# Head of a two-block fp32 kernel: input also loaded transposed, first norm applied behind the products, weight stream begun with a gate block

## The chip, the cores and the metric

The kernel runs on one core of one Trainium2 chip. The metric is the device time of one execution in microseconds (us). TensorE (PE) multiplies, ScalarE (ACT) and VectorE (DVE) work on vectors, GpSimd (POOL) does small work and issues some transfers, and SyncE (SP) issues the stream of weights.

## The reference

Two transformer blocks over 256 tokens of width 2048, all in float32. What matters here is the head of the first:

```
h   = rms_norm(x, g_mix_pre)          # x * rsqrt(mean(x*x) + eps) * g
z   = h @ w_in                        # columns: fox q,k,v,f | hgrn q,f,i,g
y1  = forgetting_attention(q, k, v, f + b)        # 8 heads
o   = hgrn2_recurrence(q_b, (1-lb)*sigmoid(-f_b), i_b, log_f)   # lb is 0 for a depth of 1
y2  = rms_norm(o, g_o) * silu(g_b)
h   = x + rms_norm(concat(y1, y2) @ w_out, g_mix_post)
```

Then come a gated feed-forward layer with a short convolution, a gated embedding, neighbourhood attention and a squared-ReLU layer. The root of a token is one number for a row of `x`, so it may be applied to the product's row (or column, where the product stands transposed) in place of the input's.

## The kernel before

All weights (some 430 MB) are read once, in 832 **slots** of at most 512 KB, fetched by SP in a fixed order into a ring of four buffers `RAW`. For exact enough products each fp32 value is split in two: ACT copies `RAW` to `HI` in the reduced format, DVE subtracts to get `LO`; PE then does three products (hi by hi, lo by hi, hi by lo). `HI` and `LO` are rings of five. ACT and DVE split slot j + 4 (`LEAD`) when they come to slot j, and ACT waits until PE is done with slot j - 1 for it. The input of a product is held transposed and in two parts too (`XT[:, k, 0]` and `XT[:, k, 1]`, k the 128-row chunk of the width).

A **block** is a set of slots that sum into one of two PSUM tensors `main0` and `main1`, in turn: `w` blocks (256 columns, 4 slots; the weights stand as the left operand) and `x` blocks (512 or 344 columns, 8 slots). `layout` lists them: hgrn f, q (`hf`, `hq`), v (`vh`), gate (`gh`), fox v (`vf`, three blocks of 344 columns, slots 32 to 55, called narrow below), then the second half of hgrn, fox q and k (`qf`, `kf`), and so on. After its last slot a block is evacuated by ACT and DVE (`evacuate`); a `w` block by `w_half` (ACT) and `w_sum` (DVE).

Work beside the stream is written out by hand in `stages`: `put(mid, j, ...)` makes every engine do a step after slot j. The recurrence of each half of the heads is done in this way: `h_abs`, `h_log`, `h_key`, `h_scan`, then eight levels of `h_decay` (DVE and POOL, then an exponential on ACT), `h_weigh` (DVE and POOL) and `h_score` (PE, and a masked copy on DVE), three slots a level, then `h_far`, `h_out`, `h_rms`, `h_gated`, `h_turn`. The score of level L reads what `h_weigh` of level L - 1 wrote. The first half starts at slot 16, the second at slot 72; the attention steps `f_score` and others go from slot 88 on.

The start is serial: x (2 MB) is loaded in four parts, ACT squares all of it, DVE and ACT make the root, both scale 512 columns each (`norm`), PE transposes them (`turn`), ACT and DVE write the two parts of `XT`, and then the first product can begin.

Of the kernel before, what the change touches and what calls it, by code (L numbers as in the profile page):

```python
# [71 lines left out]
def layout(a):  # L72
# [57 lines left out]
def stages():  # L130
# [7 lines left out]
    put(mid, 0, "norm", 0, 3)  # L138
    for kp, j in ((4, 0), (5, 0), (6, 1), (7, 1)):
        put(mid, j, "turn", 0, kp)  # L140

    for hf, j0 in enumerate((16, 72)):
# [5 lines left out]
        for lvl in range(1, 9):  # L148
            at = j0 + 7 + 3 * (lvl - 1)
# [6 lines left out]
        put(mid, j0 + 32, "h_out", hf)  # L156
        put(mid, j0 + 34, "h_rms", hf)
        put(mid, (j0 + 34, 120)[hf], "h_gated", hf)
        put(mid, (j0 + 37, 122)[hf], "h_turn", hf)
# [25 lines left out]
    put(mid, 156, "spread")  # L185
    put(mid, 155, "rb")
# [46 lines left out]
def small_banks(blocks, mid, end, early):  # L233
# [11 lines left out]
    def stage(what):  # L245
# [36 lines left out]
        elif name == "spread":  # L282
            take(("spread",), ("a_rb", 1))
# [6 lines left out]
    for kp in range(4):  # L290
        stage(("turn", 0, kp))
# [13 lines left out]
def program(nc, a):  # L305
    ctx = ExitStack()
    with ctx:
# [53 lines left out]
        XIN, NA0 = ar(12800, 2, D), ar(0, 2, D)  # L361
# [16 lines left out]
        MSKF = ar(8192, 8, 128)  # L378
        hss, hl, hr = small(32, 8), small(160, 8), small(168, 8)
# [52 lines left out]
        def freed(k):  # L432

            if k[0] in ("hf", "hq", "qf", "kf", "gate", "up", "m1"):
                return "v_wy", wth[k] + 1
            if k[0] in ("vh", "gh", "e"):
# [17 lines left out]
        wants = {k: freed(paired[i - 2]) for i, k in enumerate(paired) if i > 1}  # L454

# [32 lines left out]
        def sync_engine(eng):  # L488
# [3 lines left out]
            for t in range(2):  # L492
                for c in range(2):
                    cs = slice(c * 1024, c * 1024 + 1024)
                    L.e.dma_start(XIN[:, t, cs], xv[:, t, cs]).then_inc(S(f"d_x{t}{c}"), 16)

            def fetch(j):
# [3 lines left out]
                if j >= NRAW:  # L501
                    L.wait_ge(S("v_lo"), j - NRAW + 1)
                L.e.dma_start(dst, ap).then_inc(S(f"d_raw{i}"), 16)
# [9 lines left out]
            for j in range(len(slot)):  # L513
                fetch(j)
                if j == 140:
# [17 lines left out]
        def tensor_engine(eng):  # L533
# [10 lines left out]
            def turn(ph, kp):  # L544
                X = (NA0, H, H, H, H)[ph]
                out = take("turn", ph, kp)
                if kp == 0 and ph == 0:
                    L.wait_ge(S("d_id"), 16)
                if ph == 0:
                    L.wait_ge(S("v_n"), kp // 2 + 1)  # L550
                    L.wait_ge(S("a_n"), kp // 2 + 1)
                else:
                    L.wait_ge(S("v_h"), stream(ph - 1, kp // 2, 1))
                for q in range(2):
                    for t in range(2):
                        k = 2 * kp + q
                        x = L.e.transpose(out[:, (2 * q + t) * 128:(2 * q + t) * 128 + 128], X[:, t, k * 128:k * 128 + 128], ident)  # L557
# [12 lines left out]
            def h_score(hf, lvl):  # L570
                A, B = (Kh, Qh) if lvl == 0 else (wbuf[(lvl - 1) % 2],) * 2
                for t in range(2):
                    out = take("h_score", hf, lvl, t)
                    if lvl == 0:
                        L.wait_ge(S("a_hk"), hf + 1)
                        L.wait_ge(S("v_wy"), wth["hq", hf, 1] + 1)
# [40 lines left out]
            def f_score(h):  # L617
# [3 lines left out]
                L.wait_ge(S("v_wy"), wth["kf", hp] + 1)  # L621
# [58 lines left out]
            def spread():  # L680

                out = take("spread")
                L.wait_ge(S("v_dg"), 2)
                for t in range(2):
                    x = mm(out[:, t * 128:t * 128 + 128], ones[:, 0:128], DG[:, t, :], True, True)
# [24 lines left out]
            def x_slot(b, j, cs, out, first, last):  # L710
                hi, lo = parts(HI, j, b.n), parts(LO, j, b.n)
                A = XT if b.src == "x" else YT
                for q, c in enumerate(cs):
                    L.wait_ge(S(inputs(b, c)[0]), inputs(b, c)[1])
                    if q == 0:
# [40 lines left out]
            for kp in range(4):  # L756
                turn(0, kp)
# [20 lines left out]
        def scalar_engine(eng):  # L778
# [5 lines left out]
            def warm():  # L784
                L.wait_ge(S("v_eps"), 1)
                act(small(31, 1), epsc, ACT.Sqrt)

            def split(j):
                i, m = j % NRAW, len(slot[j][2]) * width[j]
                L.wait_ge(S(f"d_raw{i}"), 16 * (j // NRAW + 1))  # L790
                if j >= NHI:
                    L.wait_ge(S("p_use"), j - NHI + 1)
                act(HI[:, j % NHI, 0:m], RAW[:, i, 0:m], ACT.Copy).then_inc(S("a_hi"), 1)
# [5 lines left out]
            def norm(ph, c):  # L799
                cs = slice(c * 512, c * 512 + 512)  # L800
                L.wait_ge(S("v_rs"), 1)
                act(NA0[:, 1, cs], XIN[:, 1, cs], ACT.Copy, scale=rs[:, 1:2]).then_inc(S("a_n"), 1)

            def turn(ph, kp):
                out = banks[bank["turn", ph, kp]]
                L.wait_ge(S("p_xp"), turned(ph, kp))
                if ph == 0 and kp == 0:
# [17 lines left out]
            def h_abs(hf):  # L825
                L.wait_ge(S("v_wy"), wth["hf", hf, 1] + 1)
# [60 lines left out]
            def sq(inst, c):  # L887

                cs = slice(c * 512, c * 512 + 512)
                for t in range(2):  # L890
                    L.wait_ge(S("v_h"), stream(inst, c, t))
                    if c:
                        L.wait_ge(S("a_sq"), 8 + 8 * inst + 2 * c + t - 1)
# [4 lines left out]
            def root2(inst):  # L898
                root(2 + 2 * inst)

            def rb():
                L.wait_ge(S("p_rb"), 1)
                act(RB, banks[bank["spread",]][:, 0:256], ACT.Copy).then_inc(S("a_rb"), 1)

            def gate(t):
# [5 lines left out]
                L.wait_ge(S("v_rs"), 5)  # L911
# [829 lines left out]
```

## Time and profile before

| what | value |
|---|---|
| median of 3 runs | 2440.12 us (2440.0 to 2440.66) |
| the profiled execution, its own time | 2439.97 us |
| its span, first to last instruction | 2438.2 us |
| PE busy in the span | 2414.8 us, 99% |
| DVE busy, ACT busy | 1522.6 us (62%), 1221.8 us (50%) |
| transfers | 449.19 MB, mean 184 GB/s |

The time outside the span is 1.77 us. The profile's clock column (PEclk) reads full speed throughout.

### The profile page before, as it was taken

Reading aid. Unit: us, or ns where it says so; the run is one execution under the profiler, and the core shown is the slowest. Engines: PE = TensorE matmul, PEld = TensorE weight load, DVE = VectorE, ACT = ScalarE, POOL = GpSimd, SP = SyncE. Lnnn points to the kernel's source line nnn. Section 1 sums busy time; section 2 is a strip of 40 time slices with the busy share of each in tenths; the row PEclk is TensorE's granted clock in tenths of the full one; section 3 lists DMA queues with packets and bytes.
Section 4 is the critical chain, followed back from the end, with each engine's and each line's share of the span. In section 5 each row is a group of like instructions: output and inputs, shape, how many; then the busy total and the mean of one; then the engine's idle time right before and its main releaser. Section 6 shows DMA issues by size and latency. Waiting matters only on the chain.

```text
span 2438.2 us, 30545 instructions
## 1 busy us (share of the span) xinstructions
PE 2414.8 (99%) x12380; PEld 2054.9 (84%) x12380; DVE 1522.6 (62%) x1777; ACT 1221.8 (50%) x1603; POOL 111.5 (5%) x121
## 2 busy tenths in 40 slices
PE   7999999999999999999999999999999999999999
PEld 6898888788888888888877888888888888888887
DVE  5675765577657657767666666665665565554554
ACT  5554454465545545545565655554543443443442
POOL 0210410000000000000000211000000000000000
PEclk9999999999999999999999999999999999999999
DMA  8456565656655655555655655555566656566664
GB/s 245 136 163 181 147 201 168 205 160 203 199 181 177 205 180 192 196 180 183 216 191 164 190 175 174 164 164 182 180 199 191 190 187 193 183 194 193 189 196 151
DMA packets 325821, 449.19 MB, mean 184 GB/s; under 512 B 14240, under 2 KB 209056, under 8 KB 325040
## 3 DMA queue, kind: packets, MB, share of 16 engines
q1 hardware_dynamic: 323424, 438.42, 57.2%
q0 software_dynamic: 2256, 8.81, 1.2%
q8 instruction: 98, 1.61, 0.3%
q14 instruction: 43, 0.35, 0.0%
HBM read 445.08 MB, written 2.10 MB: 183 GB/s over the span
## 4 chain that ended last, share of the span: by engine, by line
PE 94%; DVE 4%; ACT 1%; issue 1%; DMA 0%; POOL 0%; SPq 0%; ACTq 0%; DVEq 0%
PE main L537 90%; PE aux L537 3%; DVE LO L1107 2%; DVE AR L1107 1%; ACT HI L782 1%; PE aux L557 1%; DVE AR L1257 0%; DMA AR<-in_x 0%; ACT AR L782 0%; PE aux L651 0%; PE aux L669 0%; DVE XT L1110 0%; POOL AR L1561 0%; DVE AR L1226 0%; DVE AR L1227 0%
## 5 line engine op out<-in xcount | busy, mean ns | idle before, releaser
L1107 DVE TENSOR_TENSOR LO<-RAW,HI 128x1024 fp32r<-128x1024 f32 (+1 forms) x832 | 1005.9, 1229 | 631.2 <-ACT HI L782 630.3
L782 ACT ACTIVATE HI<-RAW 128x1024 fp32r<-128x1024 f32 (+1 forms) x832 | 849.5, 1046 | 623.5 <-PE main L537 587.8
L537 PE MATMUL main<-XT,HI 128*128 128x512 f32 x2944 | 1037.1, 397 | 0.7 <-DVE LO L1107 0.7
L537 PE MATMUL main<-XT,LO 128*128 128x256 f32 x2944 | 825.6, 280 | 0.0
L537 PE MATMUL main<-HI,YT 128*128 128x512 f32 x2240 | 693.4, 389 | 0.0
L537 PEld LDWEIGHTS main<-XT,HI 128*128 128x128 f32 x2944 | 552.4, 188 | 132.3 <-issue 0.9
L537 PEld LDWEIGHTS main<-XT,LO 128*128 128x128 f32 x2944 | 556.2, 189 | 0.3
L537 PEld LDWEIGHTS main<-HI,YT 128*128 128x128 f32 x2240 | 420.5, 188 | 87.5
L537 PE MATMUL main<-HI,XT 128*128 128x512 f32 (+1 forms) x1472 | 456.5, 385 | 1.7 <-DVE LO L1107 1.6
L537 PE MATMUL main<-LO,YT 128*128 128x512 f32 x1120 | 435.8, 389 | 0.0
L537 PEld LDWEIGHTS main<-HI,XT 128*128 128x128 f32 x1472 | 273.8, 188 | 52.9 <-issue 1.5
L537 PE MATMUL main<-LO,XT 128*128 128x512 f32 (+1 forms) x736 | 279.9, 380 | 0.0
L537 PEld LDWEIGHTS main<-LO,YT 128*128 128x128 f32 x1120 | 210.3, 188 | 43.1
L782 ACT ACTIVATE AR<-AR 128x512 f32<-128x512 f32 (+7 forms) x187 | 108.6, 583 | 169.3 <-DVE AR L1107 84.5
L537 PEld LDWEIGHTS main<-LO,XT 128*128 128x128 f32 x736 | 138.5, 188 | 23.7
L782 ACT ACTIVATE AR<-main 128x512 f32<-128x512 f32 (+3 forms) x113 | 72.0, 638 | 150.7 <-PE main L537 150.4
L1110 DVE SCALAR_TENSOR_TENSOR AR<-main,AR 128x512 f32<-128x512 f32 (+1 forms) x125 | 86.3, 701 | 94.4 <-ACT AR L782 78.8
L1107 DVE TENSOR_TENSOR AR<-AR 128x512 f32<-128x512 f32 (+2 forms) x151 | 106.8, 714 | 25.5 <-ACT AR L782 22.4
L1110 DVE SCALAR_TENSOR_TENSOR AR<-AR,COL 128x256 f32<-128x256 f32 x176 | 74.8, 481 | 32.9 <-ACT AR L782 32.9
L537 PE MATMUL aux<-AR 128*128 128x128 f32 (+2 forms) x528 | 89.7, 316 | 4.0 <-DVE AR L1107 2.8
L537 PEld LDWEIGHTS aux<-AR 128*128 128x128 f32 x528 | 75.3, 191 | 13.4 <-issue 6.6
L782 ACT ACTIVATE AR<-AR,COL 128x256 f32<-128x256 f32 x88 | 48.2, 595 | 68.7 <-DVE AR L1107 68.7
(82 smaller groups left out, 685.6 us busy)
## 6 DMA issues: line engine op xcount, KB each, us to landing
RAW<-in_mlp_w SPq DMA_DIRECT2D x256, 512.0 KB, 4.1
RAW<-in_w_up SPq DMA_DIRECT2D x176, 512.0 KB, 4.8
RAW<-in_w_in SPq DMA_DIRECT2D x96, 512.0 KB, 3.7
RAW<-in_na_w_qkv SPq DMA_DIRECT2D x96, 512.0 KB, 4.2
RAW<-in_w_down SPq DMA_DIRECT2D x88, 512.0 KB, 4.7
RAW<-in_w_out SPq DMA_DIRECT2D x32, 512.0 KB, 4.3
RAW<-in_w_ple_gate SPq DMA_DIRECT2D x32, 512.0 KB, 4.5
RAW<-in_na_w_o SPq DMA_DIRECT2D x32, 512.0 KB, 4.2
```

The costliest lines, as they stand in the source:

```text
L537: return L.e.matmul(out, l, r, start=start, stop=stop, skip_group_check=True)
L557: x = L.e.transpose(out[:, (2 * q + t) * 128:(2 * q + t) * 128 + 128], X[:, t, k * 128:k * 128 + 128], ident)
L782: return L.e.activation(out, x, f, **kw)
L1107: return L.e.tensor_tensor(out, x, y, op)
L1110: return L.e.scalar_tensor_tensor(out, x, s, y, op0, op1, **kw)
```

## The change

The host also passes `xT`, x transposed and laid out so that a partition's row of two chunks is 2 KB. SP loads it in eight parts of 256 KB, each ahead of the weights of a slot; the first slot's weights come in two halves. ACT and DVE make `XT` straight from it with the gains alone; there are no transposes and no norm ahead of the products. The gain columns come by a small transfer that ACT itself issues.

x itself is loaded behind slots 8 to 11; ACT squares it at slots 10 and 11 (`sq0`), POOL makes the root by a power (`root0`), and PE spreads it over the partitions at slot 15 (`spread`, 0), for which ACT copies the result to `RB0`. Row-wise products (`vh`, `gh`, `vf`) get the root as ACT's scale, in two operations where there was one; transposed ones (`hf`, `hq`, `qf`, `kf`) by one more DVE product (`rooted`). The stream begins with block `gh` 0, which is kept as it is until the root is there (`gate0`). The first half's recurrence moves from slot 16 to 24, its levels and those of the second half one slot later after the first, and `f_score` to `f_out` one slot later. POOL's small loads move from the start behind slots 0, 3 and 16.

```diff
@@ layout
     w_in = a["w_in"]
+    add("x", w_in, OG, 512, allk, "x", "gh", 0)
     for hf in range(2):
...
         if hf == 0:
-            add("x", w_in, OG, 512, allk, "x", "gh", 0)
             for b in range(3):
@@ stages
-    put(mid, 0, "norm", 0, 3)
-    for kp, j in ((4, 0), (5, 0), (6, 1), (7, 1)):
-        put(mid, j, "turn", 0, kp)
+    put(mid, 0, "first_loads")
+    put(mid, 3, "more_loads")
+    put(mid, 10, "sq0", 0)
+    put(mid, 11, "sq0", 1)
+    put(mid, 11, "root0")
+    put(mid, 15, "spread", 0)
+    put(mid, 15, "rb", 0)
+    put(mid, 16, "gate0")
+    put(mid, 16, "last_loads")
-    for hf, j0 in enumerate((16, 72)):
+    for hf, j0 in enumerate((24, 72)):
...
-            at = j0 + 7 + 3 * (lvl - 1)
+            at = j0 + 8 + 3 * (lvl - 1)
...
-        for what, j in (("f_decay", j0 - 6), ("f_score", j0 + 1), ("f_norm", j0 + 2), ("f_turn", j0 + 4), ("f_out", j0 + 6)):
+        for what, j in (("f_decay", j0 - 6), ("f_score", j0 + 2), ("f_norm", j0 + 3), ("f_turn", j0 + 5), ("f_out", j0 + 7)):
@@ sync_engine
             for j in range(len(slot)):
+                if j < 4:
+                    turned_input(j)
                 fetch(j)
+                if j in (3, 4):
+                    turned_input(2 * j - 2)
+                    turned_input(2 * j - 1)
+                if 8 <= j < 12:
+                    input_rows((j - 8) // 2, j % 2)
@@ tensor_engine
+                    if j == 0 and q == 0:
+                        L.wait_ge(S("v_x0"), 1)
+                        L.wait_ge(S("v_l0"), 1)
@@ scalar_engine
+            def turned_input(kp, q):
+                k = 2 * kp + q
+                L.wait_ge(S("d_g0"), 16)
+                L.wait_ge(S(f"d_t{kp}"), 16)
+                act(XT[:, k, 0, :], XTR[:, k, :], ACT.Copy, scale=COL[:, P_MIX + k:P_MIX + k + 1]).then_inc(S("a_x0"), 1)
...
+            def sq0(t):
+                for c in range(2):
+                    L.wait_ge(S(f"d_x{t}{c}"), 16)
+                    xs = XIN[:, t, c * 1024:c * 1024 + 1024]
+                    act(xs, xs, ACT.Square, scale=MEAN, accum_out=ss2[:, t, 2 + c:3 + c]).then_inc(S("a_s0"), 1)
@@ vector_engine
+            def rooted(b, dst, n):
+                L.wait_ge(S("a_rb"), 1)
+                L.wait_ge(S("v_wy"), wth[b.what] + 1)
+                tt(dst, dst, bc(RB0, 1, n), ALU.mult).then_inc(S("v_ws"), 1)
```

How the engines' orders change is shown at three places. First ACT, from its first instruction; `d_x`, `d_raw`, `d_t`, `d_g0` and `d_w0` are transfers' semaphores (x, a slot, a part of xT, the gains, the first half slot). Before:

```order
L782 ACTIVATE AR<-AR 128x512 [waits d_x00]
L782 ACTIVATE AR<-AR 128x512
L782 ACTIVATE AR<-AR 128x512 [waits d_x01]
...
L782 ACTIVATE AR<-AR 128x2 [waits v_ms]
L782 ACTIVATE AR<-AR 128x512 [waits v_rs]
L782 ACTIVATE AR<-AR 128x512
L782 ACTIVATE HI<-RAW 128x1024 [waits d_raw0]
L782 ACTIVATE XT<-aux,COL 128x256 [waits d_col,p_xp]
```

The same place after:

```order
L1125 DMA COL<-in_cols 128x16
L802 ACT_TABLE_LOAD
L802 ACTIVATE AR<-AR 128x1 [waits v_eps]
L802 ACTIVATE XT<-AR,COL 128x256 [waits d_t0,d_g0]
L802 ACTIVATE HI<-RAW 128x512 [waits d_w0]
L802 ACTIVATE XT<-AR,COL 128x256
L802 ACTIVATE HI<-RAW 128x512 [waits d_raw0]
L802 ACTIVATE XT<-AR,COL 128x256 [waits d_t1]
L802 ACTIVATE XT<-AR,COL 128x256
L802 ACTIVATE HI<-RAW 128x1024 [waits d_raw1]
```

Eleven instructions ahead of the first split (eight squares, the root and two scalings) are gone, and the split of slot 0 stands in two halves. Second PE, from its first instruction; before:

```order
L557 MATMUL aux<-CST,AR 128x128 [waits a_n,v_n,d_id]
L557 MATMUL aux<-CST,AR 128x128 x7
L557 MATMUL aux<-CST,AR 128x128 [waits a_n,v_n]
L557 MATMUL aux<-CST,AR 128x128 x7
L537 MATMUL main<-XT,HI 128x512 [waits v_lo,v_xl]
```

and after:

```order
L562 MATMUL main<-HI,XT 128x512 [waits v_l0,v_x0]
L562 MATMUL main<-LO,XT 128x512
L562 MATMUL main<-HI,XT 128x512 x2
L562 MATMUL main<-LO,XT 128x512
L562 MATMUL main<-HI,XT 128x512
L562 MATMUL main<-HI,XT 128x512 [waits v_lo,v_xl]
```

The 32 transposes (16 here, 8 behind each of slots 0 and 1) are gone. Third DVE in the second half's recurrence, from the first level's decay to the fox block `qf` 0 (`128x256x2` is level 1, `128x128x4` level 2). Before:

```order
L1107 TENSOR_TENSOR AR<-AR 128x512 [waits v_wy,a_hx]
L1107 TENSOR_TENSOR LO<-RAW,HI 128x1024 [waits a_hi]
L1107 TENSOR_TENSOR AR<-AR 128x256x2
...
L1107 TENSOR_TENSOR AR<-AR 128x128x4
L1107 TENSOR_TENSOR LO<-RAW,HI 128x1024 [waits a_hi]
L1107 TENSOR_TENSOR AR<-AR 128x128x4 [waits a_hx]
L1110 SCALAR_TENSOR_TENSOR AR<-main,AR 128x512 [waits a_wt,a_n,v_n]
L1107 TENSOR_TENSOR LO<-RAW,HI 128x1024 [waits a_hi]
```

and after:

```order
L1144 TENSOR_TENSOR AR<-AR 128x512 [waits v_ws,a_hx]
L1144 TENSOR_TENSOR LO<-RAW,HI 128x1024 [waits a_hi] x2
L1144 TENSOR_TENSOR AR<-AR 128x256x2
...
L1144 TENSOR_TENSOR AR<-AR 128x128x4
L1147 SCALAR_TENSOR_TENSOR AR<-main,AR 128x512 [waits a_wt]
L1144 TENSOR_TENSOR AR<-AR 128x512 [waits v_wy]
L1144 TENSOR_TENSOR LO<-RAW,HI 128x1024 [waits a_hi]
L1144 TENSOR_TENSOR AR<-AR 128x128x4 [waits a_hx]
```

One more split stands ahead of level 1, and the evacuation of `qf` 0 is followed by the product with the root and stands ahead of the wait for the exponential.

## Rows read from the trace of the kernel before

**Rows 1.** Waits of PE, all of the span: us in total, times, longest.
```profile
PE aux L557 <- ACT AR L782: 12.5, 1, 12.5
```
**Rows 2.** Timeline of the start: start us, us, instruction [idle before, releaser].
```profile
0.73 1.81 SPq L495 DMA_DIRECT2D AR<-in_x  x4
...
4.87 0.63 ACT L782 ACTIVATE AR<-AR 128x512 f32<-128x512 f32 x1 [2.65 <-DMA AR<-in_x]
...
7.99 0.63 ACT L782 ACTIVATE AR<-AR 128x512 f32<-128x512 f32 x1 [0.48 <-DMA AR<-in_x]
...
9.57 0.63 ACT L782 ACTIVATE AR<-AR 128x512 f32<-128x512 f32 x1 [0.24 <-DMA AR<-in_x]
...
12.53 3.65 PE L557 MATMUL aux<-CST,AR 128*128 128x128 f32 x16 [12.53 <-ACT AR L782]
...
16.04 0.52 PE L537 MATMUL main<-XT,HI 128*128 128x512 f32 x1
...
25.22 0.48 PE L537 MATMUL main<-XT,HI 128*128 128x512 f32 x1
```
**Rows 3.** Half a microsecond of PE on the aux banks: window, busy (x), clock, DMA share, GB/s.
```profile
13.00:13.50 0.50, 0.50 (x4) 1.00 1.05 338
```
**Rows 4.** Transposes of line L557 from 12 to 17 us: ns min/median/max, first and last start.
```profile
L557 PE MATMUL aux<-CST,AR x16: 421/421/448, 12.5 to 15.8; 128*128 128x128 f32 x16
```
**Rows 5.** Transfers from 0 to 20 us: GB/s in 40 slices, issues with us to landing.
```profile
GB/s 0 0 0 66 262 254 205 246 377 426 402 393 426 410 344 279 324 360 377 389 385 369 352 374 363 342 338 402 393 389 383 375 424 387 361 371 348 299 100 14
...
BF<-in_b_fox_f POOLq DMA_DIRECT2D x1, 4.0 KB, 3.1
```
**Rows 6.** Groups of instructions from 26 to 60 us: count, busy us, mean ns, idle before.
```profile
L1107 DVE TENSOR_TENSOR LO<-RAW,HI 128x1024 fp32r<-128x1024 f32 x14 | 17.1, 1224 | 11.9 <-ACT HI L782 11.9
L782 ACT ACTIVATE HI<-RAW 128x1024 fp32r<-128x1024 f32 x13 | 13.8, 1060 | 12.5 <-PE main L537 12.4
L1110 DVE SCALAR_TENSOR_TENSOR XT<-aux,COL,XT 128x256 fp32r<-128x256 f32 x4 | 1.7, 477 | 0.0
L782 ACT ACTIVATE XT<-aux,COL 128x256 fp32r<-128x256 f32 x4 | 1.5, 470 | 0.0
```
**Rows 7.** Pieces of the chain that ended last: start us, us, what.
```profile
146.18 1.78 PE aux L537 x16
147.97 1.90 PE main L537 x12
...
487.47 0.87 PE aux L557 x8
...
1708.33 2.74 PE main L537 x12
```
**Rows 8.** Every idle of PE behind 25.22 and before 430 us, in the timeline.
```profile
94.35 2.02 PE L537 MATMUL aux<-AR 128*128 128x128 f32 x16 [0.97 <-DVE AR L1107]
...
127.82 0.42 PE L537 MATMUL main<-HI,XT 128*128 128x344 f32 x1 [0.27 <-DVE LO L1107]
...
136.01 0.40 PE L537 MATMUL main<-HI,XT 128*128 128x344 f32 x1 [0.48 <-DVE LO L1107]
...
144.02 0.43 PE L537 MATMUL main<-HI,XT 128*128 128x344 f32 x1 [0.32 <-DVE LO L1107]
...
152.82 1.13 PE L537 MATMUL aux<-AR 128*128 128x128 f32 x8 [1.08 <-DVE AR L1107]
...
250.78 2.02 PE L537 MATMUL aux<-AR 128*128 128x128 f32 x16 [0.77 <-DVE AR L1107]
...
279.89 0.46 PE L537 MATMUL aux<-AR 128*128 128x128 f32 x2 [1.22 <-DVE AR L1257]
```
**Rows 9.** Timeline of DVE: one split in each of two levels, and kf 0's sum.
```profile
134.46 1.41 DVE L1107 TENSOR_TENSOR LO<-RAW,HI 128x688 fp32r<-128x688 f32 x1 [1.85 <-ACT HI L782]
...
142.56 1.40 DVE L1107 TENSOR_TENSOR LO<-RAW,HI 128x688 fp32r<-128x688 f32 x1 [1.85 <-ACT HI L782]
...
279.12 0.68 DVE L1110 SCALAR_TENSOR_TENSOR AR<-main,AR 128x512 f32<-128x512 f32 x1
```

More of the change, by code:

```diff
@@ L184, in stages @@
         put(mid, j + 3, "root2", inst)
-    put(mid, 156, "spread")
-    put(mid, 155, "rb")
+    put(mid, 156, "spread", 1)
+    put(mid, 155, "rb", 1)
     for j, *what in ((446, "xq", 0, 0), (447, "xq", 1, 0), (448, "xq", 1, 1), (450, "turn", 3, 4), (451, "turn", 3, 5),
@@ L282, in stage @@
         elif name == "spread":
-            take(("spread",), ("a_rb", 1))
+            take(("spread",) + rest, ("a_rb", rest[0] + 1))
         elif name == "e" and rest[1] == 0 and rest[0] % 2 == 0:
@@ L544, in turn @@
             def turn(ph, kp):
-                X = (NA0, H, H, H, H)[ph]
                 out = take("turn", ph, kp)
[L547 to L553, printed above, removed]
+                L.wait_ge(S("v_h"), stream(ph - 1, kp // 2, 1))
                 for q in range(2):
@@ L678, in n_out, with spread @@
                 mm(out[:, 0:256], VN[:, 1, h * 128:h * 128 + 128], P[:, 1, :], False, True).then_inc(S("p_no"), 1)
-            def spread():
-                out = take("spread")
-                L.wait_ge(S("v_dg"), 2)
+            def spread(n):
+                out = take("spread", n)
+                L.wait_ge(S("d_cst"), 16)
+                L.wait_ge(S("v_dg"), 2 * n + 2)
                 for t in range(2):
-                    x = mm(out[:, t * 128:t * 128 + 128], ones[:, 0:128], DG[:, t, :], True, True)
+                    x = mm(out[:, t * 128:t * 128 + 128], ones[:, 0:128], (DG0, DG)[n][:, t, :], True, True)
                 x.then_inc(S("p_rb"), 1)
@@ L792, in split @@
                     L.wait_ge(S("p_use"), j - NHI + 1)
+                if j == 0:
+                    act(HI[:, 0, 512:m], RAW[:, 0, 512:m], ACT.Copy).then_inc(S("a_hi"), 1)
+                    return
                 act(HI[:, j % NHI, 0:m], RAW[:, i, 0:m], ACT.Copy).then_inc(S("a_hi"), 1)
@@ L898, in root2, with rb @@
             def root2(inst):
[L899 to L903, printed above, removed]
+                root(1 + 2 * inst)
+            def rb(n):
+                L.wait_ge(S("p_rb"), n + 1)
+                act((RB0, RB)[n], banks[bank["spread", n]][:, 0:256], ACT.Copy).then_inc(S("a_rb"), 1)
             def gate(t):
@@ L1017, in evacuate @@
                     if k[1] == 3:
-                        root(1)
+                        root(0)
                 elif k[0] == "gate":
@@ L1068, in evacuate @@
                     if nb == 3:
-                        root(5)
+                        root(4)
                 elif k[0] == "m1":
@@ L1073, in evacuate @@
                     two_parts(k[2], HD[m % 4], 22 + m)
[L1075 to L1090 removed]
+            L.e.dma_start(COL[:, 0:16], a["cols"][:, 0:16]).then_inc(S("d_g0"), 16)
+            warm(ACT.Silu)
+            for j in range(LEAD):
                 split(j)
@@ L1414, in evacuate @@
                     L.wait_ge(S("d_bf"), 16)
-                    tt(LS, out[:, :, 336:344], bc(BF[:, :], 1, 2), ALU.add).then_inc(S("v_fx"), 1)
+                    L.wait_ge(S("g_r0"), 1)
+                    for t in range(2):
+                        x = stt(LS[:, t, :], out[:, t, 336:344], rs[:, t:t + 1], BF[:, :], ALU.mult, ALU.add)
+                    x.then_inc(S("v_fx"), 1)
                     L.wait_ge(S("a_fx"), 3)
@@ L1521, in vector_engine @@
             L.e.memset(mhalf, -0.5).then_inc(S("v_eps"), 1)
-            L.wait_ge(S("a_sq"), 8)
-            root(0, ss2)
-            norm(0, 0)
-            norm(0, 1)
-            split(0)
-            turn(0, 0)
-            turn(0, 1)
-            norm(0, 2)
-            turn(0, 2)
-            turn(0, 3)
-            for j in range(1, LEAD):
+            for j in range(LEAD):
                 split(j)
@@ L1615, in n_root, with first_loads, more_loads, last_loads @@
                 L.e.tensor_tensor(rsn, mst, mhalf, ALU.pow).then_inc(S("g_rt"), 1)
+            def first_loads():
+                L.wait_ge(S("p_use"), 1)
+                load("d_go", GO[:, :], row_bc(a["g_hgrn_out"]))
+                load("d_id", CST[:, 0:128], a["cst"][:, 0:128])
+                load("d_bf", BF[:, :], row_bc(a["b_fox_f"]))
+            def more_loads():
+                L.wait_ge(S("p_use"), 4)
+                load("d_cst", CST[:, 128:C_END], a["cst"][:, 128:C_END])
+            def last_loads():
+                L.wait_ge(S("p_use"), 16)
+                load("d_col", COL[:, 16:P_END], a["cols"][:, 16:P_END])
+                load("d_msk", MSKF, a["masks"])
+                L.wait_ge(S("d_msk"), 16)
+                L.e.tensor_copy(MSK[:, :, :], MSKF).then_inc(S("g_msk"), 1)
+            def root0():
+                L.wait_ge(S("v_eps"), 4)
+                L.wait_ge(S("v_m0"), 1)
+                L.e.tensor_tensor(rs, ms, mhalf, ALU.pow).then_inc(S("g_r0"), 1)
             def bias0():
```

209 lines of the change are left out of this document (114 added, 95 removed).

## The prediction

> **What bounds the kernel now.** I read the table of waits first, then the timeline of the start, the chain that ended last, and the timeline of PE filtered for idle time. PE is what everything waits for. Its one large idle is the first 12.5 us, waiting for ACT [rows 1]; behind 25.22 us it idles seven times more before 430 us, 5.11 us in all [rows 8], and little after. So a change of the start is worth what it moves PE's first products, plus or minus what it does to those seven waits.
>
> The start reads as a chain [rows 2]: x is issued at 0.73, its first part landed at 4.87, the last at 9.57 (ACT's squares start then), transposes begin at 12.53, the first product at 16.04. Between and behind slots 0 and 1 PE does 16 more transposes and waits for splits, and slot 2 begins at 25.22. From there PE has its products back to back. **The number to compare is the start of slot 2: 25.22.**
>
> **The start after.** PE needs for its first products the first chunk of xT, the gains, and half of slot 0's weights. These are 256 KB and 256 KB at the head of SP's queue, together as much as the first part of x, which landed at 4.87 [rows 2]. The gains are 8 KB on ACT's own queue; the row nearest is the 4 KB load, 3.1 us from issue to landing [rows 5], so they are there at about 3.9 and hide beside the weights. From 4.87: ACT's copy of 512 columns (0.6, as its squares of 512 in [rows 2]), DVE's subtraction of 512 (some 0.68, [rows 9] for an operation of that size): the first product starts at about 6.15. The other three steps of slot 0 (one more chunk of XT on each engine, 0.4 each, and the second half) end at about 7.2.
>
> Here is a cost the clock column doesn't show. The first 16 transposes came four in half a microsecond, 421 ns each, with a granted clock of 1.00 beside them [rows 3, 4]; later ones go eight in 0.87 us [rows 7]: half the pace, so PE was then in effect at 1.2 GHz, the lower of its levels, and had been idle before. It was at full pace at 16.04, 3.5 us later. After, it is products that meet this. At 2.74 us for 12 in an x slot [rows 7] one takes 0.23, at half pace 0.455. With 3.5 us of half pace from 6.15, eight products take until 9.7 and four more until 10.6. The Trainium skill, "TensorE: Matmul & The Clock Gate", Part 1, says the same of an array that was idle: it starts at 1.2 GHz and rises after sustained work, and the count of slow products varies between runs. By that page's sentence on variation the point could as well come earlier or later; the trace agrees on the half pace and has one sample of when it ends.
>
> Slot 1 waits for its split. By bytes, its weights end at 1.5 MB of the queue, as x's third part, which had landed when ACT went on at 7.99 [rows 2]. ACT 1.06 and DVE 1.22 [rows 6] make that 10.25, so it is ready when PE is at 10.6. Each further slot brings 768 KB, at 375 GB/s (most slices of [rows 5]) 2.1 us, below PE's 2.74; slot 2's weights land at about 10.3, are split at 12.6, and PE comes to it at 10.6 + 2.74 = 13.35. ACT's share of a slot is 0.94 + 1.06 and DVE's 0.95 + 1.22, both under 2.74. **So slot 2 starts at 13.35 in place of 25.22: 11.9 us gained.** Not to the gain belongs the new `spread`: two products of 128 columns in fp32, by the transposes' 0.87 for eight passes four passes or 0.44 us. **Net 11.4.**
>
> The Trainium skill, "DMA: Bandwidth & Descriptors", Anatomy of one DMA, puts a transfer at 2.0 us plus its bytes at 436 GB/s. By that (an estimate from the page) half a megabyte issued at 0.73 is there at 3.9 and the sum would be 12.4; the trace's own 4.87 for the same bytes is not as quick, and I take the trace.
>
> **What moves beside it, at no cost.** The squares (2048 columns behind each of two slots, as much as four of the old 0.63 [rows 2], 2.5 us), POOL's power, the doubled evacuations of `vh`, `gh` and `vf`, eight DVE products of 0.68 and four of 1.2. In wide slots ACT was idle 12.5 us and DVE 11.9 of 34 [rows 6], and both run up to four slots (11 us) ahead, so nothing waits; where that cover is gone, in the narrow slots, each microsecond on DVE is one on PE. DVE is held in `root0` until ACT and POOL are through, some 4.5 us behind the end of slot 10, and queued behind it is the split of slot 16, which PE wants 13.7 us behind that end.
>
> **The seven waits.** *First half* [rows 8]: the first five, 3.12 us. Score 1 was 0.97 late. From the end of the last q block to score 1 PE had ten wide slots, after it has eight wide and three narrow ones: 10 x 2.75 = 27.5 against 22.0 + 5.7 [rows 7] = 27.7, and the narrow split saves a third of ACT's and DVE's time, 0.7 together. I take 0.3 left (0 to 0.9). Then DVE's round of one level in narrow slots takes 142.56 - 134.46 = 8.1 [rows 9], 1.85 of it a wait for ACT, where PE has 3 x 1.90 + 1.78 = 7.5 [rows 7] and some tenths of pipeline: what it lost was 0.27 to 0.48 a level. Before, levels 4 to 7 fell on narrow slots and three waits of splits came of it; now levels 1 to 7 do. With the lead of splits used up in level 1, five waits of some 0.4 follow, 2.1, and the 1.08 at `h_far`. Sum 3.5: **0.4 more than before.** Against it stands that the gate block's evacuation (1.2 us of DVE, two table loads on ACT) no longer falls amid the levels; from both sides the five are 0.8 to 3.
>
> *Second half* [rows 8]: the last two, 1.99 us. Score 1 at 250.78 was 0.77 late and now has one slot, 2.75 us, more, while DVE's own work to that point grows by nothing. The fox score at 279.89 waited for kf 0's evacuation, whose sum stands at 279.12 for 0.68 [rows 9], though the table names another line of DVE. It too is a slot later; DVE has 1.4 more to do (two products with the root), but one masked copy (1.3) and one split fewer stand before it. Both waits go: **2.0 less.**
>
> **Sum.** 11.4 - 0.4 + 2.0 = 13.0. Span 2438.2 - 13.0 = 2425.2; its own time was 1.77 above its span, so 2427.0; the median of the runs stands 0.15 over the profiled one: **2427.1 us.** Two outcomes differ for a measurement of this kernel from about 0.2%, 4.9 us.
>
> **Rivals.**
> *The supply is short.* To slot 12 some 11.7 MB are to come (13 slots, xT, x and 0.7 MB of POOL's), wanted split by 40.6 us, so landed by 38.3. At 375 GB/s they are there at 34 to 35; at 320 GB/s at 39.8. For it speaks that the slices fall to 279 to 342 at times [rows 5] and that x's four parts stand between slots 8 to 12, against it the mean. It costs 1.5 us at 320 and 5 at 290: 2428.5 to 2432. Chance 0.14.
> *PE stays slow for longer.* With twice the 3.5 us of half pace slot 2 starts at 15.1: 2428.9. Nothing in this trace decides when it ends. Chance 0.14.
> *The levels lose more.* The root's products and doubled evacuations sit in the narrow rounds: if each of seven levels costs 0.9 and the second half's waits stay, 3 + 2 us: 2430 to 2432. Chance 0.12.
> *The change does not do what it says:* the start is bound by something else, as if slot 0 still waited for 2 MB (9.57 and two splits, slot 2 at 20): 2433 to 2438, within 0.2%. The first part's landing at 4.87 speaks against it. Chance 0.02.
> *Slower.* The mechanism is again supply, for all slots to 24: wide slots' 512 KB and x's extra would need 13 us of waits, so a rate below some 230 GB/s over 40 us. The trace had 375 in its full slices. Over 2445: chance 0.02.
> My forecast, both parts as reckoned within 2 us: 0.56.
>
> **Range.** 2423.5 (no wait left in the first half, 3.5 us) to 2432 (one of the first three rivals in full). That leaves some 0.15 out. Faster by over 0.2% is all that ends below 2435.2: 0.96; within: 0.02; slower: 0.02.
>
> **What would show it.** First product at 6 to 6.5; products of slot 0 at twice the spacing for some 3.5 us; slot 2 at 13 to 13.7; no idle of PE from slot 2 to slot 31; ACT not waiting on `RAW` at slots 8 to 12; five or so waits of 0.3 to 0.5 on splits between slots 37 and 52; none at the second half's score 1 and at the first fox score. Wrong it would be if the first part of xT lands past 6 us, if PE waits for splits in slots 3 to 15, or if new waits of PE stand behind slot 90, where every DVE product with the root lies.

## The result and the profile after

| what | before | after |
|---|---|---|
| median of the runs beside each other | 2440.39 us (2440.0 to 2440.83, 4 runs) | 2427.85 us (2427.8 to 2428.32, 4 runs) |
| ratio, 95% interval | | 0.9949 [0.9932, 0.9966] |
| span of the profiled execution | 2438.2 us | 2426.0 us |
| PE busy, DVE busy, ACT busy | 2414.8, 1522.6, 1221.8 us | 2412.5, 1533.1, 1216.4 us |

The change makes the kernel 12.5 us faster (0.5%). Of the 12.2 us by which the span is shorter, 2.3 are busy time of PE and 9.9 its idle time. The longest wait of PE after, from the table of waits over all of the span (us in total, times, longest), answers to [rows 1]:

```profile
PE main L562 <- DVE LO L1144: 9.2, 6, 6.1
```

The wait of 12.5 us for ACT is one of 6.1 us for DVE. The timeline of the start, ACT's, SP's, DVE's and PE's rows (start us, us, instruction, idle before it and what ended it), against [rows 2]:

```profile
0.73 0.41 ACTq L1125 DMA_DIRECT2D COL<-in_cols  x1
...
1.18 0.42 SPq L519 DMA_DIRECT2D RAW<-in_w_in  x1
...
4.17 0.51 ACT L802 ACTIVATE XT<-AR,COL 128x256 fp32r<-128x256 f32 x1 [1.50 <-DMA COL<-in_cols]
4.64 0.63 ACT L802 ACTIVATE HI<-RAW 128x512 fp32r<-128x512 f32 x1
...
5.30 0.69 DVE L1144 TENSOR_TENSOR LO<-RAW,HI 128x512 fp32r<-128x512 f32 x1
...
9.40 1.23 DVE L1144 TENSOR_TENSOR LO<-RAW,HI 128x1024 fp32r<-128x1024 f32 x1 [1.62 <-ACT HI L802]
...
6.14 0.77 PE L562 MATMUL main<-HI,XT 128*128 128x512 f32 x1 [6.14 <-DVE LO L1144]
6.70 0.63 PE L562 MATMUL main<-LO,XT 128*128 128x512 f32 x1
...
10.54 0.46 PE L562 MATMUL main<-LO,XT 128*128 128x512 f32 x1
...
30.15 0.39 PE L562 MATMUL main<-XT,HI 128*128 128x512 f32 x1
```

The first product starts at 6.14, the products follow 0.43 us apart until 10.54 and 0.23 us apart behind it. The clock column says 1.00 beside both paces:

```profile
9.00:10.00 1.00, 1.00 (x4) 0.81 (x3) 0.60 (x1) 1.00 (x3) 0.00 (x0) 1.00 1.06 408
...
11.00:12.00 1.00, 1.00 (x6) 0.78 (x6) 0.96 (x3) 1.00 (x3) 0.46 (x1) 1.00 1.05 387
```

(window; then the busy time and count of PE, of its weight loads PEld, of DVE, ACT and POOL; PEclk, DMA share, GB/s). The first of the two isn't a reading. The column starts from 1.00 and takes off what the trace's records of the granted clock say, and the first such record begins at 10.66 us here and at 16.12 in before, which is where the pace doubles in either; ahead of it the trace says nothing of the clock. So at a kernel's start the spacing of the products has to be read, and the full speed that the column shows there is no evidence. The block `gh` 0 ends at 30.15; six wide slots of 2.72 us, 16.3, before that is the start of slot 2: 13.8, where it was 25.22.

Every idle of PE of 0.2 us or more behind that and before 430 us, in the timeline, answers to [rows 8]; beside them the score products of three levels:

```profile
126.25 0.42 PE L562 MATMUL main<-HI,XT 128*128 128x344 f32 x1 [0.31 <-DVE LO L1144]
128.24 1.95 PE L562 MATMUL aux<-AR 128*128 128x128 f32 x16
134.35 0.42 PE L562 MATMUL main<-HI,XT 128*128 128x344 f32 x1 [0.39 <-DVE LO L1144]
136.35 1.95 PE L562 MATMUL aux<-AR 128*128 128x128 f32 x16
142.46 0.43 PE L562 MATMUL main<-HI,XT 128*128 128x344 f32 x1 [0.39 <-DVE LO L1144]
144.46 1.95 PE L562 MATMUL aux<-AR 128*128 128x128 f32 x16
151.57 0.42 PE L562 MATMUL main<-HI,XT 128*128 128x344 f32 x1 [1.38 <-DVE LO L1144]
...
159.51 1.13 PE L562 MATMUL aux<-AR 128*128 128x128 f32 x8 [0.24 <-DVE AR L1144]
```

There is none in the second half. A level takes 136.35 - 128.24 = 8.11 us. Without a wait it takes 7.45 (experiment 7), so one that reads 0.39 costs 0.66. Of the 0.27 on top, 0.10 is the first product behind the idle time, after which the next comes 0.26 us later, where others come 0.16 apart; the rest is the tail of the product ahead, which in a row without a wait the next one overlaps.

**Where the 12.2 us of the spans are.** Slot 2 starts 25.22 - 13.8 = 11.4 us sooner. `spread` takes 0.37 of it back. The eight slots behind the gate block take 22.60 us and the next eight 22.26: 0.34 more, and I have no cause for that. The first half's waits cost 4.7 us with all that hangs on them, where they cost 4.4: 0.3 back (these two are the same slots in the kernels of experiment 7, which have no such waits: slots 32 to 55 take 63.40 us in after and 58.70 in e10_exp_later; slots 24 to 55 take 88.45 in before and 84.07 in e12_before_exp). Slot 64, in the second half, starts 10.04 us sooner, so that 0.3 us stay without a row. From there to slot 120 another 2.2 us are gained.

### The profile page after: what moved, and what is told of

Its sections match the earlier page's. It is cut to its first block, busy times and chain, and to the rows that moved or that the text cites. A ratio compares the mean times of both kernels' runs of the same rounds, so it can differ in the third digit from the quotient of the medians.

```text
span 2426.0 us, 30523 instructions
## 1 busy us (share of the span) xinstructions
PE 2412.5 (99%) x12352; PEld 2052.1 (85%) x12352; DVE 1533.1 (63%) x1788; ACT 1216.4 (50%) x1596; POOL 110.6 (5%) x122
## 4 chain that ended last, share of the span: by engine, by line
PE 97%; DVE 2%; ACT 0%; issue 0%; DMA 0%; POOL 0%; DVEq 0%; ACTq 0%
PE main L562 92%; PE aux L562 3%; DVE LO L1144 1%; PE aux L575 1%; DVE AR L1144 0%; ACT HI L802 0%; PE aux L669 0%; PE aux L687 0%; DVE AR L1316 0%; DVE XT L1147 0%; DMA COL<-in_cols 0%; DVE AR L1147 0%; PE aux L653 0%; DVE AR L1285 0%; DVE AR L1286 0%
## 5 line engine op out<-in xcount | busy, mean ns | idle before, releaser
L1144 DVE TENSOR_TENSOR LO<-RAW,HI 128x1024 fp32r<-128x1024 f32 (+2 forms) x833 | 1007.7, 1230 | 615.4 <-ACT HI L802 614.0
L802 ACT ACTIVATE HI<-RAW 128x1024 fp32r<-128x1024 f32 (+2 forms) x833 | 850.2, 1045 | 623.9 <-PE main L562 577.0
L802 ACT ACTIVATE AR<-main 128x512 f32<-128x512 f32 (+1 forms) x107 | 66.7, 624 | 140.1 <-PE main L562 140.1
L1144 DVE TENSOR_TENSOR AR<-AR 128x512 f32<-128x512 f32 (+3 forms) x163 | 117.3, 726 | 26.0 <-ACT AR L802 22.4
```

The source lines that it names most:

```text
L802: return L.e.activation(out, x, f, **kw)
L1144: return L.e.tensor_tensor(out, x, y, op)
```

## The experiments

Times are medians, against 2427.85 us for after and 2440.2 to 2440.9 for before. PE's start differs by some tenths from profile to profile of kernels whose code is the same up to there, and the pace of its first products too (last section), so of two profiles the stretches are compared, and of two kernels the medians.

**1. The second half's places back one slot (e1_second_back).**

```diff
-            at = j0 + 8 + 3 * (lvl - 1)
+            at = j0 + 8 - hf + 3 * (lvl - 1)
...
-        for what, j in (("f_decay", j0 - 6), ("f_score", j0 + 2), ("f_norm", j0 + 3), ("f_turn", j0 + 5), ("f_out", j0 + 7)):
+        for what, j in (("f_decay", j0 - 6), ("f_score", j0 + 1), ("f_norm", j0 + 2), ("f_turn", j0 + 4), ("f_out", j0 + 6)):
```

> The changed kernel (2427.85 us) with the later places undone for the second half of the heads and the fox steps alone: levels, h_out, h_rms and f_score to f_out of those one slot earlier again, as in the kernel before. Theory: the two waits of the second half (0.77 and 1.22 us of idle before) were removed by this slot; both come back, and since DVE now has the products with the root ahead of the fox score, 2.0 to 3.0 us: 2430 to 2431. Rival (the waits went because the start is no longer serial, and DVE is further ahead for all that follows): no change, 2427.6 to 2428.2.

Measured: 2432.55 us (2432.27 to 2432.72), 4.7 slower than after. PE's first rows of the fox score, and the windows around them, with the clock behind POOL's count:

```profile
270.96 0.46 PE L562 MATMUL aux<-AR 128*128 128x128 f32 x2 [2.39 <-issue]
...
272.05 1.49 PE L562 MATMUL aux<-CST,AR 128*128 128x256 f32 x4
```

```profile
270.00:272.00 2.00, 1.04 (x6) 1.01 (x7) 1.97 (x4) 0.00 (x0) 0.00 (x0) 0.94 0.68 235
272.00:274.00 2.00, 2.00 (x9) 1.77 (x8) 0.59 (x1) 1.31 (x2) 0.18 (x1) 0.50 0.35 74
274.00:276.00 2.00, 2.00 (x10) 1.73 (x10) 1.28 (x1) 0.69 (x1) 2.00 (x2) 0.71 0.56 196
```

Where four fox products of 256 columns take 0.81 us in after (271.49), here they take 1.49. What is late is `kf` 0's product with the root, the operation that the change adds:

```profile
269.46 0.67 DVE L1147 SCALAR_TENSOR_TENSOR AR<-main,AR 128x512 f32<-128x512 f32 x1
270.16 0.69 DVE L1144 TENSOR_TENSOR AR<-AR 128x512 f32<-128x512 f32 x1
```

So two things weren't as expected. Score 1 did not wait: ACT's last operation of `h_log` comes 5.1 us behind the start of slot 72, where in before it came 6.4 us behind it, as ACT loads one table less (1.28 us) ahead of it, and that is more than the 0.77 it was late (read from the traces; no run tests the table load alone). And the fox score's wait is 2.39 us, after which the granted clock stood at 0.50, the 1.2 GHz level, from 271.8 to 275.2 us; the fox score takes 4.72 us instead of 2.99. 2.39 + 1.73 = 4.1. The rest lies at the start: in this profile the half pace lasted longer and slot 2 began at 14.77, 0.9 later than in after. What follows: with the root's product on `kf`, the fox step's one slot more is needed, and worth more than before.

**2. Before with only these places one slot later (e2_before_shifted).** The reverse edit, in before.

> The kernel before (2440.4 us) with only the places of the second half and of the fox steps one slot later, nothing else. Theory: 2.0 us faster, 2438.4, with no idle of PE between 234 and 430 us. Rival, as above: no change, 2440.4.

Measured: 2438.68 us (2438.0 to 2439.15) against 2440.9 (2439.76 to 2441.19) beside it: 2.2 faster. The interval of the ratio, 0.9982 to 1.0001, just takes in no change, but the two sets of times don't overlap, and in the profiles the stretch from slot 80 to slot 120 alone is 2.2 us shorter. PE's waits for evacuations and masked copies fall:

```profile
PE aux L537 <- DVE AR L1107: 2.0, 2, 1.1
```

The line for the fox score (1.22 us) and one of three waits here (2.8 us) are gone; no idle stands between 160 and 330 us. The term of 2.0 is right, and it is independent of the start.

**3. Dummy products ahead (e3_warm).** Ten products of a memset tile into a free bank from 0.99 us on, for nothing but to occupy PE.

```diff
+            L.wait_ge(S("g_w"), 1)
+            for i in range(10):
+                mm(banks[3][:, 0:128], AR[:, 8192:8320], AR[:, 8192:8320], True, True)
```

> The changed kernel with ten products of 128 columns on constants (into an aux bank nothing else has begun to use) ahead of the first product, so that PE is busy from about 1 us. Theory: the ten products of slot 0 at half pace come from PE having been idle, and cost 2.2 us; the dummies take 0.44 each at half pace and end at about 5.5, the rise comes before or near 6.1, and 1.5 to 2.2 us are saved: 2425.7 to 2426.4, if slot 1's split (10.6 us) then makes PE wait: slot 0 would end at 8.9, so 1.6 us of the gain could be given back there and only 0.5 be left: 2427.4. I hold the second number for the likelier, as the split of slot 1 ends at 10.5 in the changed kernel's trace. Rival (the slow pace belongs to the first products of a kernel whatever ran before): no change.

Measured: 2427.81 us (2427.73 to 2428.21), no different from after. PE's timeline:

```profile
0.99 4.63 PE L562 MATMUL aux<-AR 128*128 128x128 f32 x20 [0.99 <-POOL AR L1721]
6.86 0.47 PE L562 MATMUL main<-HI,XT 128*128 128x512 f32 x1 [1.23 <-DVE LO L1147]
7.16 0.40 PE L562 MATMUL main<-LO,XT 128*128 128x512 f32 x1
...
11.46 0.47 PE L562 MATMUL main<-HI,XT 128*128 128x512 f32 x1 [1.61 <-DVE LO L1147]
```

The half pace is gone (0.40 for what took 0.63), and slot 1's split takes its place: 1.61 us of wait. The first product stands 0.7 us later than in after, because the loads of this profile landed later. So the half pace cost at most some 0.4 us that the supply wouldn't have cost: in after slot 1's split was done at 9.40 + 1.23 = 10.63, and PE came to it at 11.07.

**4. The dummy products longer and slot 1 in halves (e11_warm_halved, e13_warm_to_start).** Both have the later exponentials of experiment 7 too, so they stand against its 2423.14 us. Slot 1's split is cut as slot 0's is, the edit in ACT (DVE and PE alike):

```diff
-                    if j == 0:
-                        L.wait_ge(S("d_w0"), 16)
-                        act(HI[:, 0, 0:512], RAW[:, 0, 0:512], ACT.Copy).then_inc(S("a_h0"), 1)
+                    if j < 2:
+                        L.wait_ge(S("d_raw1") if j else S("d_w0"), 16)
+                        act(HI[:, j, 0:512], RAW[:, j, 0:512], ACT.Copy).then_inc(S("a_h0"), 1)
```

> The kernel with the later exponentials (e10_exp_later), with the ten dummy products ahead (as in e3_warm) and with slot 1 split in halves as slot 0 is, so that its first products wait for the first half alone; nothing left out. Theory (with TensorE at full pace from its first product, the end of slot 1's split is what slot 1 waits for; in e3_warm that split ran from 9.0 to 11.3 us, of which the second halves are 1.1 us): slot 1 begins about 1.0 us sooner than in e3_warm, 0.7 us sooner than in e10_exp_later, and the time is 2422.0 to 2422.8. Rival (slot 1's second half or slot 2 is then waited for, or the landing of the loads sets it all): 2422.9 to 2423.6, with the wait one slot further on.

Measured: 2423.03 us (2422.65 to 2423.84): no gain that shows. The same ten dummies did not bring full pace in this profile; with 0.62 us of idle behind them the first products ran at half pace:

```profile
6.25 0.77 PE L562 MATMUL main<-HI,XT 128*128 128x512 f32 x1 [0.62 <-DVE LO L1152]
```

That put my reading of experiment 3 in doubt, so thirteen dummies, to leave no idle at all:

> The kernel of e11_warm_halved with thirteen dummy products ahead in place of ten, so that at 0.46 us each they end at 7.0 us and leave no idle time ahead of the first product (in e11_warm_halved 0.62 us stood there, and the first products ran at half pace until 10.2 us; in e3_warm 1.23 us stood there, and they ran at full pace). Nothing is left out. Theory (the idle stretch ahead of the first product is what makes the half pace): the first product starts by 7.1 us at full pace, slot 1 at 10.3 us, and the gate block ends 0.6 to 0.7 us sooner than in e11_warm_halved, 2422.2 to 2422.6. Rival (the half pace ends at a moment of its own, between 9 and 12.5 us in the traces so far, whatever TensorE did ahead of it): the first products run at half pace from 7.0 us, and the time is 2423.0 to 2424.0.

```profile
0.99 5.23 PE L562 MATMUL aux<-AR 128*128 128x128 f32 x26 [0.99 <-POOL AR L1726]
5.98 0.47 PE L562 MATMUL main<-HI,XT 128*128 128x512 f32 x1
...
10.14 0.47 PE L562 MATMUL main<-HI,XT 128*128 128x512 f32 x1 [1.17 <-DVE LO L1152]
...
13.34 0.47 PE L562 MATMUL main<-HI,XT 128*128 128x512 f32 x1 [0.23 <-DVE LO L1152]
```

Measured: 2423.57 us (2422.29 to 2423.89). In the profile the pace is full from the first product, 13 dummies took 5.23 us where ten had taken 4.63, and the gate block ends at 29.78, 0.23 sooner than with ten; the time is in the rival's range, the pace is not the rival's. The gain ends at slot 1's first half (10.14, from a load that ACT waits for) and again at slot 2. In the medians nothing of it shows. The records of the clock fit: with dummies the first one begins at 6.03 us (e3_warm), 10.19 (e11_warm_halved) and 5.35 (e13_warm_to_start), in the first and the last ahead of the first product, and in the second where the pace doubles. Without dummies it begins between 9.15 and 12.69 in the other kernels with the change. The mechanism (PE's earlier work decides its pace) is borne out in two of three profiles; that it always works is not shown. Nor is the idle time ahead of the first product what decides: it was 1.23 us in e3_warm, at full pace, and 0.62 in e11_warm_halved, at half.

**5. Slot 0 whole (e4_first_whole).** The halves of the first slot undone in all four engines.

> The kernel after, with slot 0 loaded and split whole (512 KB in one, no halves). Theory: ScalarE and VectorE each take their whole 1.2 us step on it, and the second half of the load is waited for, so the first product starts 1.0 to 1.5 us later, at 7.2 to 7.6 us; of this the half pace of the first products (it ended at 10.5 us, by the time and not by the number of products) gives some back, so the time is 2428.3 to 2429.3. Rival (half pace lasts for a number of products or for so long after the first): the whole 1.0 to 1.5 us shows, 2428.9 to 2429.4. Rival (the supply of slot 1 sets the end of slot 0, as with the dummy products ahead): under 0.3 us.

Measured: 2429.23 us (2428.76 to 2429.44), 1.4 slower. Its first product starts at 7.88, 1.74 us later, and in the profile the gate block ends 0.92 us later: half pace ended 3.0 us behind the first product instead of 4.4. The halving is worth about 1.4 us; the split between first product and half pace is within what profiles differ by.

**6. The supply (e8_rows_early).** x by rows behind slots 2 to 5.

```diff
-                if 8 <= j < 12:
-                    input_rows((j - 8) // 2, j % 2)
+                if 2 <= j < 6:
+                    input_rows((j - 2) // 2, j % 2)
```

> The kernel after, with the four loads of x by rows (2 MB) queued behind slots 2 to 5 instead of behind slots 8 to 11. Theory (the first slots come at 370 to 390 GB/s and are used about as fast, so that the place of the rows is what keeps the supply ahead): each of the four 512 KB loads puts the slots behind it 1.4 us later, the slack of the early slots is 1 to 3 us, so TensorE waits 2 to 4 us at the LO of slots 4 to 7, and the time is 2430 to 2432. Rival (the transfers are well ahead at these slots too): no wait, 2427.5 to 2428.2.

Measured: 2432.85 us (2432.33 to 2433.05), 5.0 slower. That is more than the 2430 to 2432 expected. PE's timeline has three waits, at slots 4, 5 and 6, and ACT's has the landing that causes the first:

```profile
21.23 0.47 PE L562 MATMUL main<-HI,XT 128*128 128x512 f32 x1 [1.73 <-DVE LO L1144]
25.24 0.47 PE L562 MATMUL main<-HI,XT 128*128 128x512 f32 x1 [1.05 <-DVE LO L1144]
29.40 0.47 PE L562 MATMUL main<-HI,XT 128*128 128x512 f32 x1 [1.15 <-DVE LO L1144]
```

```profile
18.76 1.06 ACT L802 ACTIVATE HI<-RAW 128x1024 fp32r<-128x1024 f32 x1 [2.98 <-DMA RAW<-in_w_in]
```

The supply is close behind PE in the early slots: in after the split of slot 5 is done at 19.41 + 1.22 = 20.6 us, and PE comes to it at 13.8 + 3 x 2.72 = 22.0. The rows' place behind slot 8 is part of the gain. In after the transfers ran at 373 GB/s over the first slots (window, last column), where the forecast had 375:

```profile
4.00:18.00 14.00, 11.86 (x43) 9.63 (x44) 10.82 (x18) 10.36 (x18) 1.78 (x3) 1.00 1.03 373
```

**7. The narrow stage (e6_vf1_later, e5_no_root_products, e10_exp_later, e12_before_exp).** Two of the narrow waits differ from what I forecast: 1.38 at 151.57 instead of 0.4, and 0.24 at `h_far` instead of 1.08. ACT's and DVE's rows ahead of the 1.38:

```profile
147.35 1.06 ACT L802 ACTIVATE AR<-AR 128x1024 f32<-128x1024 f32 x1 [5.05 <-DVE AR L1144]
148.31 0.97 ACT L802 ACTIVATE AR<-main,AR 128x344 f32<-128x344 f32 x2
149.17 2.11 ACT L802 ACTIVATE HI<-RAW 128x688 fp32r<-128x688 f32 x3
```

```profile
141.00 1.41 DVE L1144 TENSOR_TENSOR LO<-RAW,HI 128x688 fp32r<-128x688 f32 x1 [1.85 <-ACT HI L802]
...
149.98 1.53 DVE L1144 TENSOR_TENSOR LO<-RAW,HI 128x688 fp32r<-128x688 f32 x1 [2.73 <-ACT HI L802]
```

The evacuation of `vf` 1 stands between the exponential and the split, so DVE waits 2.73 us in place of 1.85. e6_vf1_later moves that evacuation behind the split of slot 52:

```diff
+                    if j == 48:
+                        evacuate(late)
...
-                evacuate(b)
+                if b.what == ("vf", 1):
+                    late = b
+                else:
+                    evacuate(b)
```

> The changed kernel with ACT's evacuation of the block vf 1 one slot later in ACT's order, behind the split of slot 52. Theory: the 1.38 us of idle at 151.57 is 1.0 more than its neighbours (0.31 to 0.39) because the two operations of this evacuation (0.97 us) stand between an exponential and the split that DVE waits for; behind the split they cost nothing, 1.0 us saved: 2426.9. Rival (the lead of the splits is used up there anyway): the wait stays over 1.2 us, 2427.8.

Measured: 2427.99 us (2427.85 to 2428.85). The one wait shrank and the next grew:

```profile
151.73 0.42 PE L562 MATMUL main<-HI,XT 128*128 128x344 f32 x1 [0.39 <-DVE LO L1149]
160.53 1.13 PE L562 MATMUL aux<-AR 128*128 128x128 f32 x8 [1.09 <-DVE AR L1149]
```

0.39 + 1.09 against 1.38 + 0.24: the sum is the same. It isn't this operation's place that counts but the length of DVE's round. e5_no_root_products takes the root's products out of DVE, so that this kernel leaves the roots of `hf`, `hq`, `qf` and `kf` out of its results:

```diff
-                tt(dst, dst, bc(RB0, 1, n), ALU.mult).then_inc(S("v_ws"), 1)
+                L.e.memset(small(220, 1), 0.0).then_inc(S("v_ws"), 1)
```

> The kernel after, with VectorE's 12 products by the roots of the first norm replaced by a memset of one element, so that hf, hq, qf and kf leave their roots out. Theory (they lie in wide slots where VectorE stands still anyway): under 0.3 us, 2427.5 to 2428.1. Rival (they delay splits or the h_ chain of the first half, 0.7 us each): the waits of the narrow stage shrink by up to 0.7 us or the wide slots by 0.3 us, 2426.8 to 2427.4.

Measured: 2427.94 us (2427.91 to 2428.0). They cost nothing, where they stand. e10_exp_later attacks the wait of 1.85 us itself: ACT issues each level's exponential one slot later, behind the next split.

```diff
+            held = []
...
+                    for what in held:
+                        beside(what)
+                    held = [what for what in mid.get(j, []) if what[0] == "h_decay"]
                     for what in mid.get(j, []):
-                        beside(what)
+                        if what[0] != "h_decay":
+                            beside(what)
```

> The kernel after, with ScalarE's exponential of every h_decay issued one slot later, behind the split of that slot (both halves; nothing left out). Theory (a round of VectorE and ScalarE per level sets the narrow stage: the split of one slot stands behind an exponential that itself waits for both differences, so VectorE stands 1.85 us per level): the HI of that split comes before the exponential, VectorE's wait of 1.85 us shrinks under 1 us, the waits of TensorE at the LO of slots 45 to 57 and at h_far go (4.7 us with their ramps), and the time is 2423 to 2425. Rival (the waits come from the supply of LO as such, or the weighing that comes later then holds the score products): the waits move to the score products or stay, and the time is 2427 to 2429.

Measured: 2423.14 us (2422.84 to 2423.51), 4.7 faster than after and the fastest kernel here with e11_warm_halved: 0.9929 [0.9914, 0.9944] of before. The split and the exponential on ACT, the subtraction on DVE, and PE's levels:

```profile
139.30 0.78 ACT L802 ACTIVATE HI<-RAW 128x688 fp32r<-128x688 f32 x1
139.97 1.06 ACT L802 ACTIVATE AR<-AR 128x1024 f32<-128x1024 f32 x1
```

```profile
140.11 0.88 DVE L1149 TENSOR_TENSOR LO<-RAW,HI 128x688 fp32r<-128x688 f32 x1 [1.14 <-ACT HI L802]
```

```profile
127.11 1.95 PE L562 MATMUL aux<-AR 128*128 128x128 f32 x16
134.56 1.95 PE L562 MATMUL aux<-AR 128*128 128x128 f32 x16
```

The split's HI now stands ahead of the exponential, DVE's subtraction runs beside it, a level takes 7.45 us, and PE has no idle left in this stage. Slots 32 to 55 are 4.70 us shorter than in after, and that is the whole gain. The same edit in before:

> The kernel before with only ScalarE's exponential of every h_decay issued one slot later, behind the split of that slot; nothing left out. Theory (the waits of the narrow stage are VectorE's wait behind that exponential, in before as in after; they cost before 4.55 us with their ramps, and the second half 2.0 us at places that are one slot early): the narrow stage's waits go, the second half's score waits stay or grow by up to 1 us, and the time is 2435 to 2437. Rival (the narrow waits of before come from something else, since it has one slot less between chain and score): 2439 to 2441.

Measured: 2433.34 us (2433.1 to 2433.89), 6.8 faster than before; both expectations were too high. The narrow waits went, as the theory has it. So did those of the second half, which I had expected to stay: DVE stood 1.7 to 3.0 us a level there in before, behind the split that waits for the exponential, and at most 0.9 in the same levels now, and is in time for score 1 and for the fox score even one slot early. The waits of PE that are left, beside the first one, are those of the start and some of under 0.6 us each at 1325 to 1333 us, which every kernel here has:

```profile
PE main L537 <- DVE LO L1112: 0.9, 2, 0.6
PE aux L557 <- DVE AR L1131: 0.7, 1, 0.7
```

So one edit of ACT's order ends all seven waits of [rows 8], and some 2 of the 12.5 us that the change gives could be had without it. With the later exponentials on both sides the change is worth 2433.34 - 2423.14 = 10.2 us.

## Why the prediction was right

Forecast 2427.1, measured 2427.85, by the steps of the prediction:

- **The first product at 6.15:** it came at 6.14, by the chain given, in which two small errors cancelled. The first part of xT was there, and the half slot's weights, issued at 1.18, took 3.4 us, so that they landed at 4.6 and not at 4.87; from there to the product it was 1.5 us and not 1.28. The gains were not hidden: forecast for 3.9, they landed only just before 4.17, where ACT's first operation on XT waited for them. That put this operation level with the weights' landing, and it cost nothing that shows.
- **Half pace for 3.5 us:** the mechanism is right, the size is a draw. It lasted 4.4 us in after, ten products and not eight, and 3.0 to 6.1 in the others. In after it made slot 2 start at 13.8 instead of 13.35. This is the mis-sized term, 0.5 us. With the 0.34 us at slots 8 to 15 and the 0.3 without a row it is more than the 0.75 us by which the time is above the forecast; the two halves and `spread` came out 0.4 better than forecast. That the total is so near is in part luck. The rival of a half pace twice as long, priced at 2428.9, was drawn in the profiled run of e6_vf1_later: 6.1 us, slot 2 at 15.0, 2428.85 us, where that kernel's other three runs took 2427.85 to 2428.03.
- **Slot 1 ready when PE is:** yes, and with so little to spare that full pace gains nothing that the medians show (experiments 3 and 4).
- **Hidden work:** right for the squares, POOL's power and the evacuations (no idle from slot 2 to score 1) and for the root's products (e5_no_root_products).
- **First half, +0.4 us:** near in sum, +0.3. Its parts were not: score 1 did not wait, four splits waited and not five, one of them 1.38 us, and `h_far` 0.24 us. The idle times as the profile reads them even fell, from 3.12 to 2.71 us; the forecast added up such readings, and each wait costs some 0.3 us more than its reading. One level's round sets the sum, and e6_vf1_later shows that a place in it only moves where the wait appears.
- **Second half, -2.0 us:** right (2.2; alone 2.2). For score 1 the reason was only half of it: by the trace of experiment 1 one table load less would have been enough.
- **Rivals:** the supply was not short, but in slots 1 to 6 a split was done only 0.4 to 2.2 us before PE came to it. PE did stay slow for longer, by 0.9 us. The levels did not lose more. What I missed is that before's waits had a cure that has nothing to do with the change. The fixed time and rate of a transfer that the prediction takes from the Trainium skill, "DMA: Bandwidth & Descriptors", Anatomy of one DMA, are given there for transfers that GpSimd issues. Those of the start are SP's and ACT's, and the 8 KB of gains took 3.4 us.

## What to carry to other kernels

When an engine waits in a loop, read what stands ahead of it in the order of the engine that it waits for: an operation that itself waits (the exponential) ahead of one that could go at once (the split) was worth 4.7 us here, as much as all the later places of experiment 1 together. Where one wait shrinks and the next grows by as much, stop moving operations and shorten the round. A shorter start is worth what the next limit allows: here the splits of slots 1 and 2 were done only 0.4 and 1.1 us before PE came to them.

## What the runs showed of the hardware

- PE's pace behind an idle start: products of 512 columns took 0.43 us each for 4.4 us (after), 5.9 (e1_second_back), 6.1 (e6_vf1_later), 3.1 (e10_exp_later, e8_rows_early), 4.3 (e5_no_root_products), 3.0 (e4_first_whole) and 4.0 us (e11_warm_halved, in spite of its dummies), then 0.23 us. The first record of the granted clock begins within 0.2 us of that change in each of them; the column's 1.00 ahead of it is no reading. The Trainium skill, "TensorE: Matmul & The Clock Gate", Part 1, has the count of slow products vary between runs, and these traces agree: after, e1_second_back, e5_no_root_products, e6_vf1_later and e10_exp_later have the same code in their first 12 us and spread from 3.1 to 6.1 us.
- An idle time of 2.39 us was followed by a granted clock of 0.50 from 271.8 to 275.2 us (e1_second_back), which the column shows as 0.50 for one 2 us window and 0.71 for the next, and which cost 1.73 us more; idle times up to 1.73 us (e8_rows_early, at 21.23) had no such row.
- An idle time of 0.39 us ahead of narrow products cost 0.66 us.
- The gains' 8 KB took 3.4 us from issue to landing, about as long as 256 KB of weights beside them (3.5 us):

```profile
RAW<-in_w_in SPq DMA_DIRECT2D x2, 256.0 KB, 3.5
...
COL<-in_cols ACTq DMA_DIRECT2D x1, 8.0 KB, 3.4
```

- The pace of wide transposed slots differed at a clock of 1.00: 173.9 ns a product in before over slots 2 to 15, 176.6 in every kernel with the change for eight slots behind the gate block and 177.4 in e12_before_exp over slots 2 to 15. What makes it is open.
